# Gate weights of the next expert loaded into spare homes and copied into place by VectorE, with a reordered start and a reordered end

## What is computed

```python
h = _rmsnorm(x, g_norm)
proj = h @ w_in                       # 32 column tiles of 128
u, q, k, v = jnp.split(proj, ...)     # u: state space branch, q/k/v: attention
lam_bar = jnp.exp(lam * dt)           # S5 parameters, from ssm_par
b_bar = ((lam_bar - 1.0) / lam)[..., None] * b_c
...
x = x + mix @ lp['w_out']             # 16 column tiles
h = _rmsnorm(x, lp['g_ffn_norm'])
# mixture of experts: 32 experts, each row goes to 2 of them
# blocks of up to 64 rows of one expert
def expert_block(args):
    rows, e = args
    xb = h_pad[rows]
    return (jax.nn.silu(xb @ w_g[e]) * (xb @ w_u[e])) @ w_d[e]
out = x + sum over the row's two experts of gate weight * expert output
y = _rmsnorm(out, g_final)
```

## Time and profile before

| | |
|---|---|
| three runs | 2050.74, 2058.48 and 2059.72 us, median 2058.48 us |
| the profiled execution | 2055.94 us by the clock of the runs, span 2054.1 us, mean TensorE clock 0.948 |
| busy: PE, PEld, DVE, ACT, POOL | 1745.0, 1233.7, 512.2, 328.6, 288.2 us |
| bytes | 517.78 MB read from HBM, 30.91 MB written |

### The profile page before, as it was taken

How to read it: one execution, slowest core, us unless ns; L and a number is a source line. 1 busy time by engine, 2 the same in 40 slices (tenths; PEclk the granted TensorE clock), 3 DMA queues, 4 the chain that set the end, 5 groups by cost and what they waited for, 6 DMA issues and landing times.

```text
span 2054.1 us, 27081 instructions
## 1 busy us (share of the span) xinstructions
PE 1745.0 (85%) x10905; PEld 1233.7 (60%) x10906; DVE 512.2 (25%) x1102; ACT 328.6 (16%) x599; POOL 288.2 (14%) x226
## 2 busy tenths in 40 slices
PE   7999999999899999977878777777778888977880
PEld 6888888887678888854444444444444444544440
DVE  6410999535365200032000000000000000000006
ACT  4003111004632011101101010101011111101102
POOL 0681322215800000001000000000000000000000
PEclk9999999999999999988999999999898899999995
DMA  5164121337954223327999999999999597999995
GB/s 236 62 153 114 69 82 62 123 148 191 6 189 176 110 85 142 124 91 310 390 408 417 402 398 406 387 405 387 403 388 390 186 403 319 415 404 411 411 417 219
DMA packets 88900, 535.86 MB, mean 261 GB/s; under 512 B 28840, under 2 KB 37544, under 8 KB 43752
## 3 DMA queue, kind: packets, MB, share of 16 engines
q1 hardware_dynamic: 74528, 513.81, 66.8%
q0 software_dynamic: 8880, 19.17, 3.1%
q10 hardware_dynamic: 5440, 2.13, 0.6%
HBM read 517.78 MB, written 30.91 MB: 267 GB/s over the span
## 4 chain that ended last, share of the span: by engine, by line
PE 52%; DMA 38%; POOL 3%; DVE 3%; issue 2%; ACT 1%; SPq 0%; POOLq 0%; DVEq 0%; ACTq 0%
DMA arena<-w_up_in 36%; PE psum L537 35%; PE psum L825 11%; PE psum L841 2%; DMA arena<-y_rows 1%; PE psum L666 1%; PE psum L672 1%; PE psum L574 1%; DVE arena L1604 1%; PE psum L804 1%; DVE arena L1597 1%; DMA y_rows<-arena 0%; POOL arena L1065 0%; POOL arena L1068 0%; DVE arena L1612 0%
## 5 line engine op out<-in xcount | busy, mean ns | idle before, releaser
L537 PE MATMUL psum<-arena 128*128 128x260 f32 x3328 | 735.5, 384 | 17.2 <-ACT arena L863 12.3
L537 PEld LDWEIGHTS psum<-arena 128*128 128x128 f32 x3328 | 633.1, 191 | 115.8 <-issue 10.3
L825 PE MATMUL psum<-arena 128*64 128x256 f32 x4352 | 542.0, 408 | 183.1 <-DMA arena<-w_up_in 153.0
L825 PEld LDWEIGHTS psum<-arena 128*64 128x64 f32 x4352 | 341.6, 147 | 392.7 <-DMA arena<-w_up_in 177.5
L841 PE MATMUL psum<-arena 128*64 128x512 f32 x1088 | 249.9, 612 | 18.0 <-ACT arena L1028 16.1
L1590 DVE TENSOR_TENSOR arena<-arena,psum 128x256 f32<-128x256 f32 x34 | 14.3, 421 | 962.4 <-PE psum L825 962.4
L841 PEld LDWEIGHTS psum<-arena 128*64 128x64 f32 x1088 | 77.2, 140 | 168.7 <-issue 139.2
L1153 POOL DMA_INDIRECT y_rows<-arena x34 | 33.9, 996 | 987.8 <-issue 987.8
L1028 ACT ACTIVATE arena<-psum 128x256 f32<-128x256 f32 x34 | 13.1, 384 | 510.9 <-PE psum L831 510.9
L1019 ACT ACTIVATE arena<-arena 64x1024 f32<-64x1024 f32 x70 | 76.3, 1140 | 18.4 <-DMA arena<-x_rows,arena 17.8
L804 PEld LDWEIGHTS psum<-arena 64*128 64x128 f32 x560 | 64.8, 202 | 22.6 <-issue 22.5
(11 more groups left out here) (302 smaller groups left out, 1060.0 us busy)
## 6 DMA issues: line engine op xcount, KB each, us to landing
arena<-w_down_in SPq DMA_DIRECT2D x64, 2048.0 KB, 27.0
arena<-w_gate_in SPq DMA_DIRECT2D x64, 2048.0 KB, 27.9
arena<-w_up_in SPq DMA_DIRECT2D x64, 2048.0 KB
arena<-w_in_in SPq DMA_DIRECT2D x32, 1024.0 KB, 4.8
arena<-w_out_in SPq DMA_DIRECT2D x16, 1024.0 KB, 4.8
arena<-k_cache_in SPq DMA_DIRECT2D x8, 1024.0 KB, 6.7
arena<-v_cache_in SPq DMA_DIRECT2D x8, 1024.0 KB, 4.8
arena<-y_rows SPq DMA_DIRECT2D x8, 1024.0 KB, 8.1
```

Source lines behind the costliest of these rows:

```text
L537: last = mm(pair(n)[:, h, :], w(kk), rhs(kk)[:, HALF * h:HALF * (h + 1)], start=(kk == begin), stop=(kk == kn - 1 and stop))
L825: last = mm(ps[64 * h:64 * h + 64, i // 2, 0:256], xtr[:, kk, :], w[:, kk, 256 * h:256 * (h + 1)], start=(kk == 0), stop=(kk == 15))
```

## The change

At the start, `x_cols` lands in its own place `xraw` (region Q), behind the gains and the first tile of `w_in`; ScalarE scales two of the four columns of each piece, VectorE the other two, both from `xraw` into `xg`, and the squares are taken of `xraw`. The square root goes ahead of the second exponential, and VectorE's parameter work is put after `rstd` and `u_out(0)`, with a further `u_out` in it.

In the experts' stage the two gate chunks get a second home each, `wnext`. SyncE loads the gate chunks of expert e + 1 there as soon as those of expert e have been copied from there to the home `wg` that TensorE reads. VectorE makes the copies at the end of its part of each block. Where the next block is of the same expert, `newer` is 0 and the copy goes from `wg` onto itself. The regions for this come from one row buffer instead of two (`both_rows`: one gather lands on partitions 0 to 63, the next on 64 to 127) and from moved tables; the table of load counts is now made by a transpose on TensorE. At the end, the low rows are loaded later in SyncE's program and into other places, and VectorE waits for each of them apart.

```diff
@@ the start: SyncE @@
+            sp.dma_start(region("gmix", 56), t["g_cols"]).then_inc(s_gc, 16)
+            load_w(0, t["w_in"][0])
             for c in range(4):
-                sp.dma_start(xg[:, 4 * c:4 * c + 4, :], t["x_cols"][:, 4 * c:4 * c + 4, :]).then_inc(s_x[c], 16)
-                if c == 0:
-                    sp.dma_start(region("gmix", 56), t["g_cols"]).then_inc(s_gc, 16)
-                    load_w(0, t["w_in"][0])
...
+                sp.dma_start(xraw[:, 4 * c:4 * c + 4, :], t["x_cols"][:, 4 * c:4 * c + 4, :]).then_inc(s_x[c], 16)
@@ ScalarE @@
             for c in range(4):
                 act.wait_ge(s_x[c], 16)
...
+                for kk in (4 * c, 4 * c + 1):
+                    last = A(xg[:, kk, :], xraw[:, kk, :], ACT.Copy, scale=gmix[:, kk:kk + 1])
+                last.then_inc(s_xg[0], 1)
+                A(sqs[c], xraw[:, 4 * c:4 * c + 4, :], ACT.Square).then_inc(s_sq, 1)
...
             A(par[:, 2, :], par[:, 2, :], ACT.Exp).then_inc(s_lact, 1)
+            act.wait_ge(s_ss, 1)
+            A(halves(rstd), ps[:, 4:6, 0:HALF], ACT.Sqrt, bias=eps, scale=1.0 / DM).then_inc(s_root, 1)
             act.wait_ge(s_ldve, 1)
             A(tmp[2], tmp[0], ACT.Exp).then_inc(s_lact, 1)
@@ the experts: SyncE @@
-                    load_chunk({4: 4, 8: 5, 12: 1}[n], 0)
+                    load_chunk({4: 4, 8: 5, 12: 2}[n], 0)
+            sp.wait_ge(s_op, 16)
+            load_chunk(3, 0)
+            for c in range(2):
+                load_chunk(c, 0, False)
             store_x2(3)
-            sp.wait_ge(s_op, 16)
-            sp.dma_start(gtab, t["g_ffn"].rearrange("o (p k) -> (o p) k", k=16)).then_inc(s_gt, 16)
-            for i in (0, 2, 3):
-                load_chunk(i, 0)
+            sp.wait_ge(s_lgr, 1)
+            load_chunk(1, 1)
+            sp.wait_ge(s_x2st, 16 * 8)
+            load_chunk(0, 1)
+            sp.dma_start(gtab, t["g_ffn"].rearrange("o (p k) -> (o p) k", k=16)).then_inc(s_gc, 16)
             sp.wait_ge(s_tab, 1)
-            with sp.Fori(1, NE) as e:
+            with sp.Fori(1, NE - 1) as e:
                 done = sp.value_load(base_i[0:1, bass.ds(e, 1)], min_val=1, max_val=NBLK)
-                for i in range(6):
+                for i in range(2, 6):
                     sp.wait_ge(s_fr[i], done)
                     load_chunk(i, e)
+                for i in range(2):
+                    sp.wait_ge(s_copied[i], done)
+                    load_chunk(i, e + 1)
@@ the experts: TensorE @@
-                    pe.wait_ge(s_ld[i], loaded)
+                    if i < 2 and not first(n):
+                        pe.wait_ge(s_copied[i], n)
+                    else:
+                        pe.wait_ge(s_ld[i], loaded)
@@ the experts: VectorE, at the end of expert(n, j, it) @@
                 rows_turned(n + 1)
+                loaded = dve.value_load(loads_i[0:1, bass.ds(n + 1, 1)], min_val=16, max_val=16 * NE)
+                newer = dve.value_load(newer_i[0:1, bass.ds(n + 1, 1)], min_val=0, max_val=1)
+                for c in range(2):
+                    old = (at["W"], at["W"] + 12288)[c]
+                    dve.wait_ge(s_ld[c], loaded)
+                    dve.wait_ge(s_fr[c], n + 1)
+                    dve.tensor_copy(view(old, 4096), arena[:, bass.ds(newer * (ahead_at[c] - old) + old, 4096)]
+                                    ).then_inc(s_copied[c], 1)
@@ the end: SyncE @@
+            sp.wait_ge(s_copied[1], more + NE)
+            sp.dma_start(fx[4][0:NS], x2_rows[SEQ:T, 0:DM]).then_inc(s_flow, 16)
+            sp.dma_start(fg, t["g_final"].to_broadcast([P, DM])).then_inc(s_gc, 16)
             sp.wait_ge(s_sct, last_base * 16)
...
             load_y(f_low, 0, 4, s_flow)
-            sp.wait_ge(s_gdone, more + NE)
+            sp.wait_ge(s_udone, more + NE)
             for i in range(4):
-                load_y(f_low, 0, i, s_flow)
-            sp.wait_ge(s_ddone, more + NE)
-            sp.dma_start(fg, t["g_final"].to_broadcast([P, DM])).then_inc(s_gf, 16)
+                load_y(f_low, 0, i, s_x[i])
```

209 lines of the change are left out of this document (114 added, 95 removed).

## The result

| | before | changed |
|---|---|---|
| median of 8 runs each, us | 2058.42 (2050.74 to 2062.19) | 2043.76 (2040.35 to 2048.16) |
| ratio to before | | 0.9948, 95% interval 0.9931 to 0.9966 |
| span of the profiled execution, us | 2054.1 | 2041.5 |

The change makes the kernel 0.52% faster, 14.7 us by the medians and 12.6 us by the two spans. The sum of the prediction was 14.5. It is nearly right by errors that cancel, as the stages show.

The account below looks back on a forecast made before the run. The prediction took full DMA engines streaming expert weights as the bound, with gains only where they idle. Its terms, 12.6 + 2 + 0.9 - 1 = 14.5 us off the profiled 2055.9, gave 2041 us, range 2030 to 2052.

Parts of the forecast that it names:

- The stage: Experts' stage: first block and two stops gain 12.6 us together, fewer dips 2 us more.
- The two stops: At the two experts with two blocks, early gates save 11.0 us, the stream resumes 6.8 later: 4.2 us gained each.
- The first block: Expert 1's gates already loaded save 11.0 us, but up 0's load comes 6.75 us later: 4.2 us gained.
- I take nothing for either: Ahead of the first block, gather and small `g_ffn` table, with 5 and 2 us left, were reckoned to cost nothing.
- rival B: Gain hidden: first stop gives nothing, first block starts 4 us late behind five chunks; 6 us left, 2050; chance 0.20.
- Dips: Elsewhere in the experts' stage, two more queued chunks keep DMA engines from running dry: 2 us gained, ends 0 and 5.
- The copies: VectorE's 68 gate copies of 128x4096 take 2.5 us each, ends 2.3 and 4.8, hidden in the stream.
- Rival C: Copies slow the experts' weight stream: 8.5% eats the gain, 25% costs 42 us, giving 2083; chance 0.10.
- rival D: Copies hold up GpSimd's transfers at block ends; DMA engines waiting too would add 85 us, giving 2126; chance 0.02.
- The start: Up to the injection: tiles 3.4 us earlier, but TensorE waits longer and slows; loss 1 us, ends -2 and +4.
- The end: Low rows' two additions end at 2023.7 instead of 2024.6, each tile waited for apart: 0.9 us gained.
- The signs: Expected trace marks; wrong if full windows fall below 396 GB/s, have a longer period, or block 0 begins after 941.

Follow-up runs that it names:

- gates_late: Changed kernel, but the next expert's gates load only after the present expert's last block used its own, copies kept; ratio to before 0.9991.
- start_alone: Kernel before with only the change's new start (load order, scaling, root, third u tile); 2059.12 us, ratio to before 1.0041.
- experts_alone: Changed kernel with the start of before put back, keeping spare homes, copies and new end; 2041.18 us, ratio to before 0.994.

## Why the prediction was right in sum, step by step

- *The stage* was under-sized: 12.6 + 2 forecast (0.9 for the end stands apart), 23.1 measured, the term with the largest error. The error lies ahead of the first stop, where the first block's 4.2 and most of the 2 for dips stand against 13.8.
- *The two stops* I put at 4.2 each, 8.4, and the mechanism was the right one: from the first stop's second block on the changed kernel gains 9.3, and taking only the earlier load away costs 13.3 there (`gates_late`). By idle time alone the windows give 9.5 and 5.6; some 3 of that go back in a slower stream from 1640 to 1720 (393 GB/s for 407). My sum fixed the resume right (up 10.7 us into the second block, 10.6 before). What it left out is ahead of the second block: it starts 13.4 us after the start of the first block's last up products, for 15.0 in the earlier trace rows, TensorE's down products between them taking 7.09 us (granted clock 1.00 from 1720 to 1750) where they took 8.78 (clock 0.90); at the first stop they take 7.09 for 8.78 too. In `gates_late` they take 8.74 again at the second stop, at a clock of 0.83.
- *The first block* was forecast at 4.2 and gave nothing. The two chunks ahead are worth 10.4 us (4.2 MB at 404 GB/s), and the stream resumes 13.3 us into the block for 5.9 before, 7.4 later: 3.0. The block itself starts 3.0 us late. This is the step "I take nothing for either": the gather. I had reckoned when the store would land and not how long the gather takes behind two more chunks. It is the second half of rival B, at 3 of its 4 us; its first half, a first stop that gives nothing, is not what the runs show.
- *Dips*, forecast at 2: 1125 to 1600 ran at 404 GB/s for 396. All kernels with the new experts show 403 to 406 there, both with the old ones 396 and 399 (from 965 to 1600 it is 403 for 399, and 402 in `start_alone`). The chunks themselves show it: from the first load of expert 1 in the stage to the start of expert 20's last up products before the first stop there are 118 chunks in 664.7 us before and 116 in 645.7 in the changed kernel, 5.63 and 5.57 us each, which makes 8 us over 116. `gates_late` has the pace too (5.55, and 406 GB/s), so the earlier load isn't its cause. What is stays open: the order of the loads in the loop, the single row buffer and the moved regions came with the new experts, and no run parts them. With the first block's 3.0 and 1.7 for the down products at the first stop, these 8 make up the 13.8 but for 1.4.
- *The copies* were right: 2.296 us for a forecast of 2.5, hidden, and hidden even when doubled. Rival C is refuted: 404 and 406 GB/s, where it needed less than 396. Of rival D half is seen. GpSimd's scatters are held (1382 ns for 996), its gathers are not (949 ns for 978), and SyncE's stream runs at its full rate (404 and 406 GB/s). That transfers of GpSimd are held beside such copies and those of SyncE are not is the rule of the Trainium skill (SBUF — State Buffer, "SBUF: two separate sides"); the trace agrees for the scatters and the stream. The DMA engines did not stand waiting: their share is 1.01 from 1125 to 1600.
- *The start* was mis-sized and outside my bounds: -1 forecast, bounds -2 and +4, measured -6.2 (of which the new start costs 2.9 by `experts_alone`, on the kernel before by itself 7.0). Every time up to the stack was right (57.23 for 57.8, 130.85 for 130.9, 131.81 for 131.8). The step that failed is "TensorE arrives 3.4 us earlier and waits nearly 4 us": I followed the engine and left out what its arrival releases. It lets SyncE issue the next 1 MB tile 3.8 us earlier (154.52 for 158.32), ahead of the last stacked transfer, behind which the injection then comes by 8.3 instead of 4.1 us. The slower clock behind the longer gap, which I did name, adds to it: 10.39 us for the injection's first 64 matmuls, 7.65 before.
- *The end* was forecast at +0.9 and came to -1.3. The copies end where I had them (SyncE goes on 5.5 us behind the turned rows, forecast 5.6); the last two low tiles were there 23.5 us behind the turned rows, and I had 21.3. Loading the large ones first gives 6 us.
- *The signs.* Of those that I named, the gate loads during the first block of a stop, the copies' time and a long full window above 396 GB/s came true (a shorter one, 1640 to 1720, had 393). Block 0 began at 949.3, beyond the 941 that I had called a sign of being wrong (B), the first up load went out at 962.6 and not near 953, and the injection was 5 us late for the 1 us that I allowed. Judged by these, the path to the first block and the start were wrong, though the time fits.

Against the forecast the stage gave 8.5 more, the start 5.2 less, the way to the first block 3.0 less, the end 2.2 less: 1.9 less together, so 12.6 for 14.5. The total stands where the sum put it because the stage's surplus, most of it with no known cause, paid for three losses. That is luck.

## What to carry to other kernels

When a change brings an engine to a wait earlier, list what its progress releases, transfers above all, and ask what they will stand in front of: here 3.8 us won on TensorE became an injection 5 us late, because a 1 MB load overtook a small transfer on the path. What a look-ahead buffer gave at the two stops was the idle time that it fills, less what the stream then resumes later (9.3 us for 8.4 reckoned so); the 8 us of faster stream that came with it here were not foreseen and are not explained. The copies that free it cost nothing here, since VectorE was idle: 136 took no more time than 68. And a small load that is wanted early belongs ahead of large ones that are not: the table, the gathered rows and the stacked transfers each showed it.

## What the runs showed of the hardware that I had not expected

GpSimd's indirect store of 34 blocks took 996, 1382 (to 1628 in ten further kernels) and 3329 ns in the mean beside 0, 68 and 136 copies of 128x4096 on VectorE, while the gathers stayed at 978, 949 and 952 ns; SyncE's stream did not slow down (396, 404 and 406 GB/s). The first gather of 64 rows took 3.7 us from issue to use when the chunks ahead of it had been issued 26 to 27 us before, 6.1 when three of 2.1 MB had gone out over the 16 us before it, 9.0 with two more, the last of them some 2 us before it, and 10.1 with four issued in the 18 us before. TensorE's use followed ScalarE's last stacked transfer by 3.8 to 4.7 us where a 1 MB load went out 1 us or more behind it, by 6.5 where it went out 0.14 us behind, and by 6.7 to 9.0 where it went out 0.35 to 1.94 us ahead (seven kernels). TensorE's first 64 matmuls of the injection took 7.65 us behind gaps of 0.6 to 2.3 us and 9.2 to 10.4 behind gaps of 3.2 us and more.
